# Rotary partners of the grouped tiles by transfers within SBUF in place of matmuls, two-part sums of squares, and a third buffer in the state-space stage

## The chip, the cores and the metric

The kernel runs on one core of one Trainium2 chip, in one launch. The metric is device time in microseconds, a median over runs; lower is better. The kernel before took 3017.12 us (median of three runs, 3015.85 to 3017.46). Engines are named as in the profile: PE does matmuls, PEld is its weight load, DVE is VectorE, ACT is ScalarE, POOL is GpSimd, and SP is SyncE, which here only issues transfers.

## What is computed

Two blocks stand one after the other on 512 tokens of width 1024. The first is a hybrid of dilated attention, pooling and a state-space scan, with a gated feed-forward part; the second is two layers of three parallel branches (differential attention, retention, grouped-query attention). All of it is fp32 data. Cut to what the change touches:

```python
# first block, state-space branch, per chunk of 128 tokens and per head
seg = a_cs[..., :, None] - a_cs[..., None, :]
Lmat = exp(where(causal, seg, -inf))

# second block, each of two layers
gq = axial_rope(rms_norm(gq, gqa_q_norm[l]))      # 8 heads of 64: 4 tiles of 128 rows
gk = axial_rope(rms_norm(gk, gqa_k_norm[l]))      # 2 heads of 64: 2 tiles (each head twice)
def apply_rope(x, cos, sin):                      # x1, x2: the halves of a group
    return concat([x1 * cos - x2 * sin, x2 * cos + x1 * sin])   # axial: halves of 16 in groups of 32
a = rms_norm(differential_attention(...), diff_subln[l], eps=1e-5)   # mean of squares over 128
r = head_group_norm(retention(...), ret_group_norm[l])               # variance over 128
```

## The kernel before

**Tiling.** Activations lie with features on the 128 partitions and the 512 tokens along the free dimension, so a tile is 128x512 fp32. A dense product with fp32 accuracy is made of three fp32r matmuls for each pair of 128-row blocks: both operands are split into a high part and the rest (uH, uL for activations, wH, wL for weights), and the products high x high, low x high and high x low are summed in PSUM. A weight tile of eight such blocks thus takes 24 matmuls. Weights come in chunks of up to 512 KB through four slots: SP loads a chunk into wR (`load`, which first waits in `ended` until the chunk four places earlier is used up), ACT rounds it to wH (`high`, three chunks ahead of the engine's place in its order), and DVE or POOL makes wL (`low`, `low_pool`).

**PSUM.** Of the eight banks, four are for the dense products and four for all else ("misc"). Both sets are given out in turn by an order that is written out ahead of time (`order_block1`, `order_layer`), and each user waits until the user four places earlier has released the bank.

**Order.** There is no scheduler. Each engine's instructions stand in the order in which the code issues them, and they meet at semaphores. Attention steps on PE are interleaved with eight dense matmuls at a time from a list of fill work (`fill`), and ACT and DVE follow the same marks.

**State-space stage (first block, 336 to 438 us).** For each of 16 groups of four heads DVE writes a 128x512 tile `ta` (`spread`) and POOL its low part `tl`; PE multiplies both with one triangular matrix (`seg`, L2073 and L2075), ACT takes the exponential into `dec`, DVE multiplies it with the chunk's scores (L2251), and PE uses the result (L2084) in `pair`. `ta` has two buffers, and `spread(n + 1)` stands ahead of group n's product on DVE.

**The grouped stage (each layer's start, "g"; 1144 to 1190 us in layer 0, 2080 to 2125 us in layer 1).** Six tiles are made one after the other (numbered 0 to 5 here in that order): the first four by two interleaved pairs of products, the last two by single ones; then comes the product of the grouped values, gv, in two half chunks, and then the grouped attention (`gqa_*`). For each tile ACT writes the scaled raw tile (`raw`, two buffers) and its squares (`sq`), and then counts up `raw_tile`. PE then sums the squares (L2796, `ss`) and makes the rotary partner (L2801, `rot`): a matmul with a signed permutation, both on full fp32 operands. DVE multiplies raw with the cosine (L2935), the partner with the sine (L2906), adds them (L2913), and multiplies with the root that ACT made of the sum (L2917), then counts up `rope_done`. Tile x + 2 may be written to `raw` when tile x has counted; the first attention scores wait for four tiles.

**The other rotary tiles.** The eight differential tiles ("d") and the eight retention tiles ("r") of a layer get their partners by transfers from `raw` to `partner` or `sg`, issued by SP in `swap_sp` right behind the load four chunks on: four of 8 partitions each for a "d" tile, two of 64 partitions for an "r" tile. All loads and swaps stand in one queue on SP.

**Means of squares.** Behind each of the four heads of the differential (`mean`, L3137) and retention (`var`, L3295) stages, ACT squares the head's output, and PE multiplies the squares with a matrix of ones, in full fp32.

## Time and profile before

| | |
|---|---|
| median of three runs | 3017.12 us |
| the profiled execution, its own time | 3017.55 us |
| its span in the trace | 3015.8 us |
| PE busy | 2946.7 us, 98% |
| weight loads busy | 2314.4 us, 77% |
| DVE busy | 1553.5 us, 52% |
| ACT busy | 1281.3 us, 42% |
| POOL busy | 452.7 us, 15% |
| mean granted PE clock | 0.996 of 2.4 GHz |

PE is busy throughout, and a matmul's bar in the trace overlaps its neighbours' bars, so what one costs is read from the distance between starts, not from its bar. In the lists, idle time before an instruction is followed by what ended it.

### The profile page before, as it was taken

What the parts mean: (1) busy time and instruction counts of PE and PEld (TensorE: products, weight loads), DVE (VectorE), ACT (ScalarE), POOL (GpSimd) and SP (SyncE); (2) the same over time, 40 slices, a digit from 0 to 9 for tenths busy, and PEclk for the clock granted to TensorE, in tenths of its full rate; (3) what the DMA queues carried; (4) which work ended last, traced back from release to release, by engine and by line L of the source; (5) the groups of instructions that cost most, each with busy time, mean ns of one, the idle gap of its engine ahead of it and who ended that gap; (6) DMA issues with size and microseconds to landing.
All of it is one profiled execution on the core that took longest, in us unless ns stands there. A gap on an engine that the chain in (4) does not pass through costs nothing. (4 is left out here: it accounts for less than half of the span.)

```text
span 3015.8 us, 36165 instructions
## 1 busy us (share of the span) xinstructions
PE 2946.7 (98%) x13328; PEld 2314.4 (77%) x13328; DVE 1553.5 (52%) x2058; ACT 1281.3 (42%) x1889; POOL 452.7 (15%) x264
## 2 busy tenths in 40 slices
PE   7999989999999999999999999999999999999999
PEld 6776778888778786677777888887667777888887
DVE  3427767445764666655634551435655743553241
ACT  3556325333542446655544432234655544332231
POOL 5000110000100002211112122121221111212121
PEclk9999999999999999999999999999999999999999
DMA  7322213333323332122322333333222322333332
GB/s 189 89 71 63 58 47 91 98 98 98 99 87 101 96 93 72 48 72 79 102 70 84 98 96 93 97 98 98 55 61 74 98 78 77 98 93 96 97 98 91
DMA packets 466355, 264.18 MB, mean 88 GB/s; under 512 B 21275, under 2 KB 455293, under 8 KB 466209
## 3 DMA queue, kind: packets, MB, share of 16 engines
q1 hardware_dynamic: 460256, 251.14, 28.9%
q0 software_dynamic: 5952, 11.13, 1.4%
q8 instruction: 87, 1.43, 0.2%
q14 instruction: 60, 0.48, 0.0%
HBM read 254.85 MB, written 5.64 MB: 86 GB/s over the span
## 5 line engine op out<-in xcount | busy, mean ns | idle before, releaser
L759 POOL TENSOR_TENSOR wL<-wR,wH 128x1024 fp32r<-128x1024 f32 (+1 forms) x159 | 386.7, 2433 | 2167.3 <-ACT wH L723 2167.3
L723 ACT ACTIVATE wH<-wR 128x1024 fp32r<-128x1024 f32 (+2 forms) x475 | 491.2, 1034 | 412.3 <-DMA wR<-in_w_mlp_out_dram 193.9
L728 DVE TENSOR_TENSOR wL<-wR,wH 128x1024 fp32r<-128x1024 f32 (+2 forms) x316 | 381.0, 1206 | 434.6 <-ACT wH L723 408.7
L790 PE MATMUL ps<-uH,wH 128*128 128x512 f32 x1200 | 486.5, 405 | 8.5 <-POOL wL L759 5.6
L790 PE MATMUL ps<-uL,wH 128*128 128x512 f32 x1200 | 483.5, 403 | 0.0
L790 PE MATMUL ps<-uH,wL 128*128 128x512 f32 x1200 | 479.9, 400 | 0.0
L778 PE MATMUL ps<-uH,wH 128*128 128x512 f32 x976 | 384.6, 394 | 7.3 <-DVE wL L728 5.7
L778 PE MATMUL ps<-uL,wH 128*128 128x512 f32 x976 | 379.9, 389 | 0.0
L778 PE MATMUL ps<-uH,wL 128*128 128x512 f32 x976 | 379.9, 389 | 0.0
L790 PEld LDWEIGHTS ps<-uH,wH 128*128 128x128 f32 x1200 | 227.3, 189 | 73.1 <-issue 16.8
L790 PEld LDWEIGHTS ps<-uL,wH 128*128 128x128 f32 x1200 | 227.7, 190 | 59.7 <-issue 15.4
L790 PEld LDWEIGHTS ps<-uH,wL 128*128 128x128 f32 x1200 | 227.4, 189 | 59.4 <-issue 13.8
L778 PE MATMUL ps<-mH,wH 128*128 128x512 f32 x688 | 268.1, 390 | 2.1 <-DVE wL L728 2.1
L778 PE MATMUL ps<-mH,wL 128*128 128x512 f32 x688 | 267.7, 389 | 0.0
L778 PE MATMUL ps<-mL,wH 128*128 128x512 f32 x688 | 267.7, 389 | 0.0
L778 PEld LDWEIGHTS ps<-uH,wH 128*128 128x128 f32 x976 | 183.2, 188 | 54.8 <-issue 10.4
L778 PEld LDWEIGHTS ps<-uL,wH 128*128 128x128 f32 x976 | 183.2, 188 | 38.7 <-issue 1.4
L778 PEld LDWEIGHTS ps<-uH,wL 128*128 128x128 f32 x976 | 183.2, 188 | 38.4
L778 PEld LDWEIGHTS ps<-mH,wH 128*128 128x128 f32 x688 | 129.1, 188 | 29.7 <-DVE wL L728 2.9
L778 PEld LDWEIGHTS ps<-mH,wL 128*128 128x128 f32 x688 | 129.1, 188 | 26.9
L778 PEld LDWEIGHTS ps<-mL,wH 128*128 128x128 f32 x688 | 129.1, 188 | 26.7
L3563 ACT ACTIVATE mH<-msc 128x512 f32 x64 | 40.5, 632 | 236.1 <-DVEq L3607 236.1
(476 smaller groups left out, 4173.4 us busy)
## 6 DMA issues: line engine op xcount, KB each, us to landing
wR<-in_w_in_dram SPq DMA_DIRECT2D x188, 512.0 KB, 3.7
wR<-in_w_mlp_in_dram SPq DMA_DIRECT2D x64, 512.0 KB, 4.0
wR<-in_w_mlp_out_dram SPq DMA_DIRECT2D x64, 512.0 KB, 3.6
wR<-in_ffn_w_up_dram SPq DMA_DIRECT2D x44, 512.0 KB, 3.8
wR<-in_w_branch_dram SPq DMA_DIRECT2D x24, 512.0 KB, 3.4
wR<-in_w_out_dram SPq DMA_DIRECT2D x16, 512.0 KB, 3.7
wR<-in_ffn_w_down_dram SPq DMA_DIRECT2D x16, 384.0 KB, 3.2
wR<-in_ffn_w_down_dram SPq DMA_DIRECT2D x16, 320.0 KB, 3.0
```

The costliest lines, as they stand in the source:

```text
L723: st.f(st.e.activation(wH[:, slot, 0:n], wR[:, slot, 0:n], ACT.Copy), hi_ready, c + 1)
L728: st.f(st.e.tensor_tensor(wL[:, slot, 0:n], wR[:, slot, 0:n], wH[:, slot, 0:n].bitcast(F32), ALU.subtract), lo_ready, c + 1 if done is Non ...
L759: e.tensor_tensor(wL[:, slot, 0:n], wR[:, slot, 0:n], wH[:, slot, 0:n].bitcast(F32), ALU.subtract).then_inc(sem("lo_pool"), 1)
L778: ins = pe.matmul(outp, w[:, k, c0:c0 + m], x[:, k0 + k, :], start=k0 == 0 and s == 0, stop=k0 + kt == kn and s == len(steps) - 1)
L790: ins = pe.matmul(o[:, :], w[:, k, :], x[:, k, :], start=s == 0, stop=s == 3 * KD - 1)
L3563: st.f(e.activation(mHf[:, ds((4 * i + j) * S, S)], msc[:, j % 2, :], ACT.Copy), sem("hidH_ready"), x + 1)
```

## The change

It has three parts. The first kernel of this call (the state-space stage belongs to it) gets a third `ta` buffer and one `spread` more ahead. In each layer of the second block the partners of the six grouped tiles are made by transfers that SP issues, eight of 16 partitions x 512 for a tile, into the buffer that the "d" tiles use later; the sine table's sign is moved into the table, the 12 `rot` matmuls and one memset per layer go, and ACT converts one weight chunk ahead of a root for the last two tiles. And the 16 sums of squares behind the heads are made of two fp32r matmuls each (high part and rest), for which ACT writes the square once more as fp32r and DVE subtracts; the order of ACT's copies is changed with it.

```diff
@@ -135,7 +135,7 @@
         for o, q in ((0, t // 64), (32, t % 64)):
             a = table(q, 32, 10000.0)
             out[2, b + o:b + o + 32, 0] = np.cos(np.concatenate([a, a]))
-            out[2, b + o:b + o + 32, 1] = np.sin(np.concatenate([a, a]))
+            out[2, b + o:b + o + 32, 1] = np.concatenate([-np.sin(a), np.sin(a)])
     return np.ascontiguousarray(out.reshape(3, P, 2 * S).astype(np.float32))
 
 
@@ -474,8 +474,6 @@
     def post(kind, t):
         if kind != "r":
             M.add("ss", kind, t)
-        if kind == "g":
-            M.add("rot", kind, t)
 
     def posts(kind):
 
@@ -1852,9 +1850,9 @@
     btok = kb("btok", [P, 4, 256], 58)
     dec = kb("dec", [P, 4, S], 70)
 
-    ta, tl = kb("ta", [P, 2, S], 78, F32R), kb("tl", [P, 2, S], 104, F32R)
-    gtR = kb("gtR", [P, P], 108, F32R)
-    avH, avL = kb("avH", [P, 4, 16], 108.5, F32R), kb("avL", [P, 4, 16], 108.75, F32R)
+    ta, tl = kb("ta", [P, 3, S], 99, F32R), kb("tl", [P, 2, S], 105, F32R)
+    gtR = kb("gtR", [P, P], 109, F32R)
+    avH, avL = kb("avH", [P, 4, 16], 109.5, F32R), kb("avL", [P, 4, 16], 109.75, F32R)
     xdd = kb("xdd", [P, S], 82)
     prev = kb("prev", [P, D], 88)
     ytok = kb("ytok", [P, D], 92)
@@ -2070,7 +2068,7 @@
             pe.wait_ge(sem("ta_ready"), n + 1)
             g = M("seg", n)
             o = g.open(pe)
-            pe.matmul(o[:, :], gtR[:, :], ta[:, n % 2, :], start=True, stop=False)
+            pe.matmul(o[:, :], gtR[:, :], ta[:, n % 3, :], start=True, stop=False)
             pe.wait_ge(sem("tl_ready"), n + 1)
             g.close(pe.matmul(o[:, :], gtR[:, :], tl[:, n % 2, :], start=False, stop=True))
 
@@ -2163,10 +2161,10 @@
 
         def spread(n):
             c, q = n // 4, n % 4
-            if n >= 2:
-                e.wait_ge(misc_ready, M("seg", n - 2).nth)
-            st.w()
-            st.s(e.tensor_tensor(ta[:, n % 2, :].rearrange("p (h t) -> p h t", h=4),
+            if n >= 3:
+                e.wait_ge(misc_ready, M("seg", n - 3).nth)
+            st.w()
+            st.s(e.tensor_tensor(ta[:, n % 3, :].rearrange("p (h t) -> p h t", h=4),
                                  C("le").unsqueeze(1).broadcast_to([P, 4, P]),
                                  avH[:, c, 4 * q:4 * q + 4].bitcast(F32).unsqueeze(2).broadcast_to([P, 4, P]), ALU.mult))
             st.w()
@@ -2219,6 +2217,7 @@
         follow("bt", 0)
         silu_dve(st, 11)
         spread(0)
+        spread(1)
         for c in range(4):
             follow("xt", c)
             for x in range(2):
@@ -2236,8 +2235,8 @@
                 st.w()
                 g.done(st, e.tensor_tensor(cbm[:, :, :], o[:, 0:256].rearrange("p (g t) -> p g t", g=2),
                                            C("le").unsqueeze(1).broadcast_to([P, 2, P]), ALU.mult))
-            if n + 1 < 16:
-                spread(n + 1)
+            if n + 2 < 16:
+                spread(n + 2)
             if n >= 2 and n % 2 == 0:
                 pair((n - 2) // 4, (n - 2) % 4 // 2)
             if n >= 5 and q == 1:
@@ -2672,7 +2671,7 @@
 
     XB = {"d": ("dq", "dk"), "r": ("rq", "rk"), "g": ("gq", "gk")}
 
-    HALVES = {"d": (8, (0, 64)), "r": (64, (0,))}
+    HALVES = {"g": (16, (0, 32, 64, 96)), "d": (8, (0, 64)), "r": (64, (0,))}
     ROPE = {"d": 0, "r": 1, "g": 2}
 
 
@@ -2681,6 +2680,7 @@
     sq = kb("sq", [P, 2, S], 4)
     rs = kb("rs", [P, 2, S], 8)
     partner = {"d": kb("partner", [P, 2, S], 12), "r": sg}
+    partner["g"] = partner["d"]
     qk = {"g": kb("qk_g", [P, 6, S], 92), "d": kb("qk_d", [P, 8, S], 64), "r": kb("qk_r", [P, 8, S], 16)}
     cs = {"g": kb("cs_g", [P, 2 * S], 106), "d": kb("cs_d", [P, 2 * S], 88), "r": kb("cs_r", [P, 2 * S], 60)}
     vv = {"gv": kb("vv_g", [P, NT, P], 104), "dv": kb("vv_d", [P, NT, S], 80), "rv": kb("vv_r", [P, NT, S], 100)}
@@ -2697,6 +2697,10 @@
     gst, ast = stt[:, 0], stt[:, 1]
     vsum = stt[:, 0, 0:2, :].rearrange("p a (t h) -> p (a t) h", h=4)
     rstd = nrmt
+
+    onesR = kb("onesR", [P, P], 112.5, F32R)
+    aoL, rqH = kb("aoL", [P, S], 110, F32R), kb("rqH", [P, S], 110, F32R)
+    rmH = rmL = at("rmH", [P, S], F32R, END - 8192 - 2048)
     hs = kb("hs", [P, S], 44)
     rg = kb("rg", [P, 4, S], 88)
     ro = kb("ro", [P, 2, S], 96)
@@ -2785,6 +2789,18 @@
                 e.sem_inc(sem("rv_ready"), 1)
             yield
 
+    def sums_of_parts_pe(pe, g, hi, lo):
+
+        o = g.open(pe)
+        pe.matmul(o[:, :], onesR[:, :], hi, start=True, stop=False)
+        g.close(pe.matmul(o[:, :], onesR[:, :], lo, start=False, stop=True))
+
+    def square_low(st, low, x, hi):
+
+        st.w()
+        st.s(st.e.tensor_tensor(low, x, hi.bitcast(F32), ALU.subtract))
+        st.w()
+
     def rope_post_pe(pe, kind, x, l):
 
         if kind == "r":
@@ -2794,15 +2810,10 @@
         g = M("ss", kind, t, l=l)
         o = g.open(pe)
         g.close(pe.matmul(o[:, :], C("blk64"), sq[:, x % 2, :], start=True, stop=True))
-        if kind != "g":
-            return
-        g = M("rot", kind, t, l=l)
-        o = g.open(pe)
-        g.close(pe.matmul(o[:, :], C("rot_g"), raw[kind][:, x % 2, :], start=True, stop=True))
-
     def partner_in(kind, x, l):
 
-        return 16 * (l * (4 * 4 + 4 * 2) + (4 * 4 if kind == "r" else 0) + (x // 2 + 1) * (4 if kind == "d" else 2))
+        return 16 * (l * (3 * 8 + 4 * 4 + 4 * 2) + {"g": 0, "d": 3 * 8, "r": 3 * 8 + 4 * 4}[kind] +
+                     (x // 2 + 1) * {"g": 8, "d": 4, "r": 2}[kind])
 
     def swap_sp(e, kind, x, l):
 
@@ -2819,10 +2830,13 @@
 
         o = orders(l)[0]
         x = o.names[name] - SLOTS
-        for kind in HALVES:
+        for kind in ("d", "r"):
             first = o.names[kind, TILES[kind][0]]
             if first <= x < first + KD:
                 swap_sp(e, kind, x - first, l)
+
+        for t in {3: (0, 1), 4: (2, 3), 5: (4,), 6: (5,)}.get(x - o.names["g", TILES["g"][0]], ()):
+            swap_sp(e, "g", t, l)
 
     def rope_pe(pe, kind, l):
 
@@ -2882,9 +2896,13 @@
                 g.done(st, e.activation(raw[kind][:, x % 2, :], o[:, :], ACT.Copy))
             st.w()
             e.sem_inc(sem("raw_tile"), 1)
+            late = kind == "g" and x > 3
+            if late:
+                high(st, (kind, t), l)
             if norm and x > 0:
                 root(x - 1)
-            high(st, (kind, t), l)
+            if not late:
+                high(st, (kind, t), l)
             yield
         if norm:
             root(len(order) - 1)
@@ -2898,17 +2916,10 @@
 
         def finish(x):
             y = qk[kind][:, order[x], :]
-            z = raw[kind][:, x % 2, :]
-            if kind == "g":
-                g = M("rot", kind, order[x], l=l)
-                o = g.take(e)
-                st.w()
-                g.done(st, e.tensor_tensor(z, o[:, :], table[:, S:2 * S], ALU.mult))
-            else:
-                z = partner[kind][:, x % 2, :]
-                e.wait_ge(sem(f"partner_in{x % 2}"), partner_in(kind, x, l))
-                st.w()
-                st.s(e.tensor_tensor(z, z, table[:, S:2 * S], ALU.mult))
+            z = partner[kind][:, x % 2, :]
+            e.wait_ge(sem(f"partner_in{x % 2}"), partner_in(kind, x, l))
+            st.w()
+            st.s(e.tensor_tensor(z, z, table[:, S:2 * S], ALU.mult))
             st.w()
             st.s(e.tensor_tensor(y, y, z, ALU.add))
             if norm:
@@ -2939,8 +2950,6 @@
                 finish(x - 1)
             if kind == "g" and x > 1:
                 low(st, (kind, t), l)
-            if kind == "g" and x == 3:
-                st.s(e.memset(partner["d"][:, :, :], 0.0))
             yield
         finish(len(order) - 1)
 
@@ -3131,10 +3140,8 @@
             g.close(ins)
 
         def mean(h):
-            pe.wait_ge(sem("aosq_ready"), 4 * l + h + 1)
-            g = M("on", h, l=l)
-            o = g.open(pe)
-            g.close(pe.matmul(o[:, :], C("ones"), ao[:, 1, :], start=True, stop=True))
+            pe.wait_ge(sem("aosq_low"), 4 * l + h + 1)
+            sums_of_parts_pe(pe, M("on", h, l=l), rmH[:, :], aoL[:, :])
         diff_steps(score, turned, value, mean, fill)
 
     def diff_act(st, l, follow):
@@ -3160,8 +3167,9 @@
                 if h:
                     e.wait_ge(sem("b_ready"), 27 + 20 * l + 4 + h)
                 st.w()
-                st.s(e.activation(ao[:, 0, :], o[:, :], ACT.Copy))
-                g.done(st, e.activation(ao[:, 1, :], o[:, :], ACT.Square))
+                st.s(e.activation(ao[:, 1, :], o[:, :], ACT.Square))
+                st.s(e.activation(rmH[:, :], o[:, :], ACT.Square))
+                g.done(st, e.activation(ao[:, 0, :], o[:, :], ACT.Copy))
                 st.w()
                 e.sem_inc(sem("aosq_ready"), 1)
             if 2 <= u < 18:
@@ -3219,6 +3227,11 @@
                     if u == 0:
                         e.wait_ge(sem("root_ready"), 3)
                     final_scale_dve(st, u)
+            if u >= 7 and u % 4 == 3 and u < 20:
+                h = u // 4 - 1
+                e.wait_ge(sem("aosq_ready"), 4 * l + h + 1)
+                square_low(st, aoL[:, :], ao[:, 1, :], rmH[:, :])
+                e.sem_inc(sem("aosq_low"), 1)
             if u >= 8 and u % 4 == 0:
                 h = u // 4 - 2
                 follow("on", h)
@@ -3289,10 +3302,8 @@
             g.close(ins)
 
         def var(h):
-            pe.wait_ge(sem("rsq_done"), 4 * l + h + 1)
-            g = M("rn", h, l=l)
-            o = g.open(pe)
-            g.close(pe.matmul(o[:, :], C("ones"), rsq[:, :], start=True, stop=True))
+            pe.wait_ge(sem("rsq_low"), 4 * l + h + 1)
+            sums_of_parts_pe(pe, M("rn", h, l=l), rqH[:, :], rmL[:, :])
         ret_steps(score, value, var, fill)
 
     def ret_act(st, l, follow):
@@ -3316,10 +3327,9 @@
             if h >= 2:
                 e.wait_ge(sem("b_ready"), 27 + 20 * l + 8 + h - 1)
             st.w()
-            st.s(e.activation(ro[:, h % 2, :], o[:, :], ACT.Copy))
-            g.done(st, e.activation(rsq[:, :], o[:, :], ACT.Square))
-            st.w()
-            e.sem_inc(sem("rsq_done"), 1)
+            st.s(e.activation(rsq[:, :], o[:, :], ACT.Square))
+            st.f(e.activation(rqH[:, :], o[:, :], ACT.Square), sem("rsq_done"), 4 * l + h + 1)
+            g.done(st, e.activation(ro[:, h % 2, :], o[:, :], ACT.Copy))
             follow("rn", h)
             g = M("rn", h, l=l)
             o = g.take(e)
@@ -3363,6 +3373,9 @@
                 st.w()
                 e.sem_inc(sem("rsc_ready"), 1)
             follow("ro", h)
+            e.wait_ge(sem("rsq_done"), 4 * l + h + 1)
+            square_low(st, rmL[:, :], rsq[:, :], rqH[:, :])
+            e.sem_inc(sem("rsq_low"), 1)
             follow("rn", h)
             x = ro[:, h % 2, :]
             e.wait_ge(sem("rrt_ready"), 4 * l + h + 1)
@@ -3449,6 +3462,8 @@
         rest(fill.parts)
 
     def layer_dve(st, l):
+        if l == 0:
+            st.s(st.e.tensor_copy(onesR[:, :], C("ones")))
         normed_u_dve(st, u_base("normed", l), 1 + l, lambda k: lp[:, k:k + 1], 2 + 3 * l,
                      lambda: low(st, ("g", TILES["g"][0]), l))
         low(st, ("g", TILES["g"][1]), l)
```

SP, at the start of the grouped stage of layer 0, kernel before: `wR` is the weight buffer, the 128x4x128 loads are the two half chunks of gv, and the 128x8x128 ones belong to the "d" tiles.

```order
L716 DMA wR<-in_w_in_dram 128x4x128 x2
L716 DMA wR<-in_w_in_dram 128x8x128 x5
L2816 DMA partner<-raw 8x512 x4
L716 DMA wR<-in_w_in_dram 128x8x128
L2816 DMA partner<-raw 8x512 x4
```

The same place in the changed kernel:

```order
L714 DMA wR<-in_w_in_dram 128x4x128 x2
L2827 DMA partner<-raw 16x512 x16
L714 DMA wR<-in_w_in_dram 128x8x128
L2827 DMA partner<-raw 16x512 x16
L714 DMA wR<-in_w_in_dram 128x8x128
L2827 DMA partner<-raw 16x512 x8
L714 DMA wR<-in_w_in_dram 128x8x128
L2827 DMA partner<-raw 16x512 x8
L714 DMA wR<-in_w_in_dram 128x8x128 x2
L2827 DMA partner<-raw 8x512 x4
```

Forty-eight transfers have moved in between the loads of the second gv half and of the third "d" chunk, each row of them behind a wait for its tiles.

DVE, at the start of the state-space stage, before (`ta` is `spread`, `xdt` and `cbm` are the products with which a chunk begins):

```order
L1991 SCALAR_TENSOR_TENSOR xc_105<-xc_105,cvt 128x512
L2169 TENSOR_TENSOR ta<-cn,avH 128x512
L728 TENSOR_TENSOR wL<-wR,wH 128x1024
L2228 TENSOR_TENSOR xdt<-ps,dts 128x512 x2
L728 TENSOR_TENSOR wL<-wR,wH 128x1024
L2228 TENSOR_TENSOR xdt<-ps,dts 128x512 x6
L2237 TENSOR_TENSOR cbm<-ps,cn 128x256
L2169 TENSOR_TENSOR ta<-cn,avH 128x512
```

and in the changed kernel:

```order
L1989 SCALAR_TENSOR_TENSOR xc_105<-xc_105,cvt 128x512
L2167 TENSOR_TENSOR ta<-cn,avH 128x512 x2
L726 TENSOR_TENSOR wL<-wR,wH 128x1024
L2227 TENSOR_TENSOR xdt<-ps,dts 128x512 x2
L726 TENSOR_TENSOR wL<-wR,wH 128x1024
L2227 TENSOR_TENSOR xdt<-ps,dts 128x512 x6
L2236 TENSOR_TENSOR cbm<-ps,cn 128x256
L2167 TENSOR_TENSOR ta<-cn,avH 128x512
```

The second `ta` stands at the start, and each later one is one group further on than it was, at the same places.

DVE, between the scores of a differential step and the mean of the second head of layer 0, in the changed kernel (L3222 reduces the scores, `qk_r` and `sg` belong to a retention tile):

```order
L3222 TENSOR_REDUCE stt<-ps 128x1 x2
L2946 TENSOR_TENSOR qk_r<-raw_r,cs_r 128x512
L2922 TENSOR_TENSOR sg<-sg,cs_r 128x512
L2924 TENSOR_TENSOR qk_r<-qk_r,sg 128x512
L2801 TENSOR_TENSOR aoL<-ao,rmH 128x512
L2946 TENSOR_TENSOR qk_r<-raw_r,cs_r 128x512
```

L2801 is new; the rows around it stood in this order before.

## Rows read from the trace of the kernel before

**Rows 1.** The page: busy time of each engine, share of the span, instructions.

```profile
PE 2946.7 (98%) x13328; PEld 2314.4 (77%) x13328; DVE 1553.5 (52%) x2058; ACT 1281.3 (42%) x1889; POOL 452.7 (15%) x264
```

**Rows 2.** Groups by line: names, shapes, count | busy us, mean ns | idle before.

```profile
L2801 PE MATMUL ps<-raw,cn 128*128 128x512 f32 x24 | 12.2, 592 | 0.0
...
L3295 PE MATMUL ps<-nrmt,cn 128*128 128x512 f32 x16 | 8.2, 590 | 0.0
L3137 PE MATMUL ps<-ao,cn 128*128 128x512 f32 x16 | 8.2, 590 | 0.0
```

**Rows 3.** PE's waits, whole span: total us, times, longest us.

```profile
PE ps L2073 <- DVEq L2173: 5.7, 3, 2.9
PE ps L790 <- POOL wL L759: 5.6, 2, 2.8
...
PE ps L2084 <- DVEq L2253: 2.6, 2, 1.9
```

**Rows 4.** Timeline of PE, grouped stage, layer 0: start us, us, operation.

```profile
1155.79 1.02 PE L2801 MATMUL ps<-raw,cn 128*128 128x512 f32 x2
1156.65 1.02 PE L2796 MATMUL ps<-sq,cn 128*128 128x512 f32 x2
...
1157.96 0.79 PE L790 MATMUL ps<-uH,wH 128*128 128x512 f32 x1
```

**Rows 5.** Timeline of PE around the mean of a differential head.

```profile
1389.33 0.39 PE L790 MATMUL ps<-uH,wH 128*128 128x512 f32 x1
1389.55 1.02 PE L3137 MATMUL ps<-ao,cn 128*128 128x512 f32 x2
1390.50 1.13 PE L3007 MATMUL ps<-qk_d 64*128 64x256 f32 x8
```

**Rows 6.** Timeline of DVE between scores and mean, second head.

```profile
1423.52 0.69 DVE L2913 TENSOR_TENSOR qk_r<-qk_r,sg 128x512 f32<-128x512 f32 x1
```

**Rows 7.** Timeline of PE, state-space stage: two waits for `ta`.

```profile
408.14 0.50 PE L2073 MATMUL ps<-ta,gtR 128*128 128x512 f32 x1 [1.59 <-DVEq L2173]
...
421.88 0.50 PE L2073 MATMUL ps<-ta,gtR 128*128 128x512 f32 x1 [2.89 <-DVEq L2173]
```

**Rows 8.** Windows: stretch, us, busy by engine (instructions), granted clock, DMA share, GB/s.

```profile
405.00:415.00 10.00, 8.41 (x41) 6.84 (x41) 5.61 (x8) 2.55 (x4) 1.04 (x1) 0.83 0.18 53
420.00:430.00 10.00, 8.12 (x35) 6.55 (x36) 5.32 (x9) 3.03 (x5) 0.00 (x0) 0.83 0.19 52
...
2120.00:2130.00 10.00, 8.79 (x36) 6.28 (x36) 5.71 (x7) 4.09 (x9) 6.71 (x3) 0.83 0.00 0
```

**Rows 9.** By tile, SP's issues: count: least, median, longest ns.

```profile
L2816 SPq DMA_DIRECT2D partner<-raw x64: 624/625/1059, 1193.7 to 2215.8; - x64
...
L2816 SPq DMA_DIRECT2D sg<-raw_r x32: 461/564/2072, 1407.6 to 2403.0; - x32
```

**Rows 10.** Timeline of SP: first loads of the stage; swaps of a "d" tile.

```profile
1154.45 1.05 SPq L716 DMA_DIRECT2D wR<-in_w_in_dram  x2
...
1204.11 2.64 SPq L2816 DMA_DIRECT2D partner<-raw  x4
```

**Rows 11.** DMA issues: count, KB each, median us to landing.

```profile
cn<-table_consts_dram SPq DMA_DIRECT2D x1, 64.0 KB, 1.9
```

**Rows 12.** Timeline, grouped stage, layer 0: DVE and ACT.

```profile
1156.92 0.69 DVE L2906 TENSOR_TENSOR raw<-ps,cs_g 128x512 f32<-128x512 f32 x1
...
1159.22 0.69 ACT L2879 ACTIVATE raw<-ps,lp 128x512 f32<-128x512 f32 x1 [1.71 <-DVEq L2919]
...
1163.63 1.23 DVE L728 TENSOR_TENSOR wL<-wR,wH 128x1024 fp32r<-128x1024 f32 x1
```

**Rows 13.** Timeline, start of grouped attention, layer 0: DVE, then ACT, then PE.

```profile
1188.75 1.49 DVE L3105 TENSOR_REDUCE stt<-ps 128x1 f32<-128x512 f32 x2
...
1190.33 0.69 ACT L3071 ACTIVATE gpr<-ps,stt 128x512 f32<-128x512 f32 x1 [3.44 <-DVEq L3107]
...
1192.71 0.49 PE L3007 MATMUL ps<-qk_g 64*128 64x256 f32 x2
```

## The prediction

> **What bounds the kernel now.** I read the busy table first: PE is busy 98% of the span, DVE and ACT half of it [rows 1]. So PE's own order is the path nearly everywhere, a matmul taken out of it is worth its full place, and an edit on another engine counts only where PE comes to wait for it. Then the list of PE's waits: small ones, and three of them lie in stages that the change touches, 5.7 us at L2073 for `ta`, 2.6 us at L2084 for DVE's product with `dec`, and 5.6 us (twice 2.8) where the first fill matmul of a layer's grouped attention waits for POOL's low part of a weight chunk [rows 3]. Then the timelines of those places, for what is late next. The sum is made against the profiled execution (3017.55 us, 1.75 us over its span); it stands 0.4 us over the median 3017.12, so I add the differences to the median.
>
> **What a matmul costs.** In the timeline an fp32 product of 128x512 appears as two records, and the next product starts 0.86 us after it (1155.79 to 1156.65) [rows 4]. A dense fp32r matmul starts 0.22 us ahead of its successor (1389.33 to 1389.55), and the mean behind a head holds PE for 0.95 us until the next product (1389.55 to 1390.50), of which some 0.09 us is that product's own start [rows 5].
>
> **Part 1, the sums of squares.** L3137 and L3295 have 16 records each, so 16 products in all [rows 2]. Each goes from 0.86 us to two fp32r matmuls, 0.45 us: 0.41 us less, and 16 x 0.41 = 6.5 us. It needs an extra ACT pass (0.6 us) and a DVE subtraction (0.69 us, as DVE's L2913 [rows 6]) ahead of PE's product. For the second head of layer 0 the subtraction stands behind the L2913 that ends at 1424.2 [rows 6]; it would be ready near 1425.0, and PE's product comes two matmul groups later, at 1428.1. I went through all eight places of layer 0 in the same way; the tightest is the last differential head, about 1 us ahead of PE. So no wait takes the place of the gain, and I take -6.5 us, with 0 as the bound if DVE is late everywhere. Queued behind DVE's new waits are weight conversions; only the one behind the last differential head moves by much (some 8 us), and its chunk is two chunks from use.
>
> **Part 2, the first kernel.** PE waits for `ta` three times. With a third buffer and the same places on DVE, `ta` is there one group early and all three waits go. What is late next differs. At the first (the remaining 1.2 us, near 395 us) DVE works without a gap and PE waits 1.9 us for its product with `dec` a few microseconds on, the longest of the L2084 waits [rows 3]: the wait moves there, gain 0. At the second (1.6 us, 408.14) the next product has its operand, so 1.6 us is gained [rows 7]; the granted clock was 0.83 over 405 to 415 us, thus 10 x 0.17 = 1.7 us of full-speed work lost, and with PE fed it should stay up [rows 8]. I count 1.6 + 1.5 = 3.1 us. At the third (2.9 us, 421.88) [rows 7] the next half pair needs DVE's product, which comes behind one `ta` and two additions of some 0.7 us each, and holds PE again: of 2.9 us plus the 1.7 us of clock in 420 to 430 us [rows 8] I count 2.1 us. Sum -5.2 us; bounds 0 (DVE holds PE at all three) and -9 us (all waits 5.7 and both clock losses 3.4).
>
> **Part 3, the grouped partners.** Off PE go 12 products (24 records [rows 2]) of 0.86 us, 10.3 us, 5.2 us in each layer. In their place SP issues eight transfers for a tile, one after the other. The trace of before has no transfer of 16 partitions; the nearest are those of 8 partitions, median 625 ns, and of 64, median 564 ns [rows 9]. Four of the first take 2.64 us, 0.66 us apart [rows 10]. I take 0.66, as 16 is nearer to 8 than to 64; the bounds are 0.46, the shortest within SBUF, and 0.8, since single ones took 1.06 and 2.07 us [rows 9]. From issue to landing 64 KB take 1.9 us [rows 11]; for the last of a tile I take 2.1. So a tile's partner lands 7 x 0.66 + 2.1 = 6.7 us after its first issue.
>
> Now the walk through layer 0. The load ahead of the swaps is issued near 1155.1 [rows 10], so tile 0's transfers run from 1155.8 and land at 1162.5, tile 1's from 1161.1, landing at 1167.8. Before, DVE had tile 0's partner at 1156.92, and ACT wrote raw tile 2 at 1159.22 [rows 12]: 2.3 us of DVE lie between. Now raw tile 2 is written at 1164.8 to 1166.1. PE's first dense matmul started at 1157.96 behind both partners [rows 4]; now it starts 0.86 us earlier (not 1.7, as tile 1's squares are not ready sooner), and 24 matmuls, 5.8 us with the slower first, bring it to 1162.9. It needs tile 2's squares: **a new wait of 3.3 us**. Tile 5's product needs the low part of its weight chunk, which DVE makes (L728) only behind the finish of tile 1: before at 1163.63 [rows 12], now from 1170.1 to 1171.4. PE, free at 1167.2, waits until 1171.6, **another 4.4 us**. After such gaps I expect a lower clock: in layer 1 it was 0.83 over 2120 to 2130 us behind a 2.8 us wait [rows 8]; I add 1.2 us. SP goes on behind: tiles 2 and 3 land at 1173.8 and 1179.1, tile 4 at 1185.9, tile 5 at 1191.9. Those do not hold the next products for more than 0.6 us, since ACT now converts one chunk ahead of the root; and the 2.8 us wait for POOL [rows 3] goes, because PE comes late for it anyway. The first scores start at 1188.9. But DVE has tile 5 to finish ahead of the first maximum: 1191.9 + 2.2 = 1194.1, where it was 1188.75, and ACT's exponentials, which free the PSUM bank that the second scores need, end at 1196.5 instead of 1191.0 [rows 13]. PE starts those scores at 1196.7, against 1192.71 [rows 13]: **layer 0 is 4.0 us slower**, and the 5.2 us of removed products are used up. In layer 1 the same walk gives 0.5 us less, and the clock loss of before (10 x 0.17 us in 2120 to 2130 [rows 8]) mostly has its place in the new waits: +2.4 us. Together +6.4 us; at 0.46 us an issue the same walk gives about -1 us a layer, at 0.8 us some 6 us a layer more.
>
> One page of the Trainium skill speaks against this part: DMA: Bandwidth & Descriptors, section Rules for kernel authors, says to coalesce small transfers and that under 64 KB one mostly pays overhead; these are 32 KB. The same page, section Anatomy of one DMA, puts the sequencer's share at about 50 ns (for the GpSimd path): by that, an estimate, a tile's eight issues would be 0.4 us, both waits would nearly vanish, and part 3 would be worth most of its 10.3 us. The 0.66 us between starts [rows 10] is against the small share.
>
> **Sum.** -6.5 - 5.2 + 6.4 = -5.3 us, 3011.8. Waits of 2 to 4 us follow each other in the grouped stage, and a second low-clock stretch there is about as likely as not in one layer (1.7 us at the most); I round up to **3012.0 us**.
>
> **Rivals.** *(a) The transfers hide.* If SP issues them at 0.46 us, part 3 gives -2 us: 3017.1 - 6.5 - 5.2 - 2 = 3003.4 us; if an issue costs next to nothing, part 3 gives some -9 us, 2996.4 us. Range 2996 to 3006. For it: some issues within SBUF took 0.46 us; against it: the medians of 0.56 and 0.63 us [rows 9]. 0.12, of which 0.03 for the lower value. That lower value is what the page named above would give. *(b) The swap queue holds PE longer, and the kernel is slower than before.* Place: SP's queue, 48 transfers a layer. From 0.66 to 0.8 us an issue each tile comes 1.1 us later, the six in series 6 us a layer, +12: 3024 us. The point where the gain of the other parts is used up is about 0.72 us an issue (5.3 us of the 12 us that 0.14 us cost). For it: single issues of up to 1.06 and 2.07 us [rows 9]; against it the medians. The same sign comes about if two clock losses fall in each layer. 0.18, range 3017 to 3030. *(c) The first kernel gives nothing*, since DVE, not `ta`, holds PE at all three places; the L2084 wait [rows 3] shows that it does at one: 3017 us, range 3014 to 3018. 0.15. The forecast itself, 0.55, with a range of 3005 to 3017.
>
> **Range and chances.** 3003.5 to 3020.5 us leaves out most of (a) and the upper half of (b), together under 0.2. A measurement of this kernel can tell about 0.2% (6 us) from no change. Faster by more than that (under 3011.1): (a), and somewhat over half of the forecast's case, 0.41. Slower by more (over 3023.1): half of (b), 0.09. Within: 0.50.
>
> **What would show it.** In the profile of the changed kernel: L2801 and L3137/L3295 gone from PE, 32 fp32r matmuls in their place, 0.22 us apart and with no wait ahead of them (part 1). No PE wait at `seg`; a longer one at the `dec` products near 400 and 424 us, and a granted clock near 1 from 405 to 430 us (part 2). SP's 48 swaps per layer some 0.66 us apart; PE waits of 3 us ahead of the sum of squares of the third tile and of 4 us ahead of tile 5's product, released by ACT and by DVE's wL; a clock dip right there; and DVE's first maximum some 5 us later (part 3). What would make me wrong: an issue spacing under 0.5 or over 0.75 us, or low-clock stretches that come or go elsewhere.

## The result and the profile after

| | before | changed |
|---|---|---|
| median, 13 runs each | 3017.11 us (3013.93 to 3020.54) | 3022.47 us (3018.28 to 3026.57) |
| ratio, 95% interval | | 1.0018 (1.0009 to 1.0026) |
| span of the profiled execution | 3015.8 us | 3016.5 us |

The change makes the kernel 5.4 us slower, where I had forecast 5 us faster; the time is 2 us above the top of my range. The trace needs care: the profiled execution of the changed kernel took 3018.28 us, the least of its 13 runs, with a mean granted clock of 0.993; the median of the runs' clocks is 0.990. Among the 13, 0.001 of clock goes with 1.5 us. So the trace shows where the time goes, but less of it than the usual run has.

From the page of the changed kernel, the busy times (PE's is 12 us less than in [rows 1]), and then lines of the list of PE's waits (us in total, times, longest):

```profile
PE 2934.4 (97%) x13304; PEld 2311.1 (77%) x13304; DVE 1567.6 (52%) x2073; ACT 1288.7 (43%) x1905; POOL 453.1 (15%) x264
```

```profile
PE ps L788 <- DVE wL L726: 11.5, 5, 4.2
PE ps L3016 <- ACT gpr L3080: 8.2, 4, 3.8
...
PE ps L2812 <- ACTq L2898: 6.3, 2, 3.2
PE ps L2082 <- DVEq L2252: 5.8, 3, 3.2
```

Against [rows 3], the waits for `ta` and for POOL are gone. One group is new, the wait for the squares of a tile (L2898), and three have grown: for the low part of weights (L726 is DVE's `low`; 2.9 us before), for the exponentials of the first scores (L3080; 0.7 us before), and for DVE's product with `dec` (L2252; 2.6 us before). The timeline of PE in layer 0's grouped stage shows the first three of them in order (L2812 is the sum of squares, L788 dense, L3016 scores):

```profile
1149.72 1.02 PE L2812 MATMUL ps<-sq,cn 128*128 128x512 f32 x2
...
1160.64 1.23 PE L2812 MATMUL ps<-sq,cn 128*128 128x512 f32 x2 [3.15 <-ACTq L2898]
1166.12 0.79 PE L788 MATMUL ps<-uH,wH 128*128 128x512 f32 x1 [4.24 <-DVE wL L726]
1166.71 0.63 PE L788 MATMUL ps<-uL,wH 128*128 128x512 f32 x1
1167.13 0.63 PE L788 MATMUL ps<-uH,wL 128*128 128x512 f32 x1
...
1194.12 1.13 PE L3016 MATMUL ps<-qk_g 64*128 64x256 f32 x8 [3.73 <-ACT gpr L3080]
...
1201.53 1.13 PE L3016 MATMUL ps<-qk_g 64*128 64x256 f32 x8
```

```profile
1154.93 1.02 PE L2796 MATMUL ps<-sq,cn 128*128 128x512 f32 x2
...
1198.51 1.13 PE L3007 MATMUL ps<-qk_g 64*128 64x256 f32 x8
```

The second fence is the kernel before, with the same first and last event (the first sum of squares and the third scores): 43.6 us lie between them there, 51.8 in the changed kernel, so layer 0's stage costs 8.2 us more. Layer 1 costs 5.5 more (from 2090.23 to 2140.87 us, before 2090.83 to 2135.99). What releases PE is on SP and DVE (L2827 is the swap, L2922 to L2928 the finish of a tile, L3114 the maximum of the scores), with POOL's low parts (L757) below:

```profile
1150.32 10.39 SPq L2827 DMA_DIRECT2D partner<-raw  x16
...
1161.38 11.30 SPq L2827 DMA_DIRECT2D partner<-raw  x16
```

```profile
1157.08 0.69 DVE L2922 TENSOR_TENSOR partner<-partner,cs_g 128x512 f32<-128x512 f32 x1 [5.51 <-DMA partner<-raw]
...
1164.84 1.22 DVE L726 TENSOR_TENSOR wL<-wR,wH 128x1024 fp32r<-128x1024 f32 x1 [0.50 <-DVE qk_g L2928]
...
1187.06 0.81 DVE L2922 TENSOR_TENSOR partner<-partner,cs_g 128x512 f32<-128x512 f32 x1 [2.59 <-DMA partner<-raw]
1187.90 2.78 DVE L2924 TENSOR_TENSOR qk_g<-qk_g,partner 128x512 f32<-128x512 f32 x1
1190.79 0.69 DVE L2928 TENSOR_TENSOR qk_g<-qk_g,rs 128x512 f32<-128x512 f32 x1
1191.62 1.48 DVE L3114 TENSOR_REDUCE stt<-ps 128x1 f32<-128x512 f32 x2
```

```profile
1184.94 5.19 POOL L757 TENSOR_TENSOR wL<-wR,wH 128x1024 fp32r<-128x1024 f32 x2 [2.54 <-ACT wH L721]
```

Tile 0's partner is used 6.8 us after the first issue, and 16 issues take 10.39 us, 0.65 us each. The granted clock (the third column from the end), in windows of the changed kernel:

```profile
1165.00:1171.00 6.00, 4.88 (x12) 3.82 (x13) 4.69 (x5) 2.55 (x5) 1.71 (x1) 0.50 0.26 57
1190.00:1200.00 10.00, 6.28 (x30) 4.87 (x29) 7.54 (x10) 6.20 (x13) 2.51 (x2) 0.83 0.22 60
```

Behind the waits of 3.15 and 4.24 us PE has 0.50, the 1.2 GHz level, and its matmuls start 0.42 us apart (1166.71 to 1167.13) in place of 0.23.

The means are as intended, two fp32r matmuls 0.23 us apart, without a wait:

```profile
1392.58 0.39 PE L2795 MATMUL ps<-rmH,onesR 128*128 128x512 f32 x1
1392.81 0.39 PE L2796 MATMUL ps<-aoL,onesR 128*128 128x512 f32 x1
```

### The profile page after: what moved, and what is told of

It is laid out like the page before. It is cut to its first block and busy times, and to the rows that moved or that the text cites. A ratio compares the mean times of both kernels' runs of the same rounds, so it can differ in the third digit from the quotient of the medians.

```text
span 3016.5 us, 36263 instructions
## 1 busy us (share of the span) xinstructions
PE 2934.4 (97%) x13304; PEld 2311.1 (77%) x13304; DVE 1567.6 (52%) x2073; ACT 1288.7 (43%) x1905; POOL 453.1 (15%) x264
## 5 line engine op out<-in xcount | busy, mean ns | idle before, releaser
L757 POOL TENSOR_TENSOR wL<-wR,wH 128x1024 fp32r<-128x1024 f32 (+1 forms) x159 | 386.9, 2434 | 2170.8 <-ACT wH L721 2170.7
L726 DVE TENSOR_TENSOR wL<-wR,wH 128x1024 fp32r<-128x1024 f32 (+2 forms) x316 | 380.5, 1204 | 419.4 <-ACT wH L721 392.2
L788 PE MATMUL ps<-uH,wH 128*128 128x512 f32 x1200 | 486.1, 405 | 12.1 <-DVE wL L726 11.5
L788 PE MATMUL ps<-uL,wH 128*128 128x512 f32 x1200 | 481.8, 402 | 0.0
L788 PE MATMUL ps<-uH,wL 128*128 128x512 f32 x1200 | 479.6, 400 | 0.0
L776 PE MATMUL ps<-uH,wH 128*128 128x512 f32 x976 | 384.7, 394 | 7.1 <-DVE wL L726 5.6
L776 PE MATMUL ps<-uH,wL 128*128 128x512 f32 x976 | 380.0, 389 | 0.0
L776 PE MATMUL ps<-uL,wH 128*128 128x512 f32 x976 | 380.0, 389 | 0.0
L788 PEld LDWEIGHTS ps<-uH,wH 128*128 128x128 f32 x1200 | 227.8, 190 | 78.6 <-issue 16.7
L788 PEld LDWEIGHTS ps<-uL,wH 128*128 128x128 f32 x1200 | 228.0, 190 | 58.4 <-issue 13.9
L788 PEld LDWEIGHTS ps<-uH,wL 128*128 128x128 f32 x1200 | 227.3, 189 | 58.1 <-issue 12.5
L776 PE MATMUL ps<-mH,wH 128*128 128x512 f32 x688 | 268.1, 390 | 2.1 <-DVE wL L726 2.1
L776 PE MATMUL ps<-mH,wL 128*128 128x512 f32 x688 | 267.7, 389 | 0.0
L776 PE MATMUL ps<-mL,wH 128*128 128x512 f32 x688 | 267.6, 389 | 0.0
L776 PEld LDWEIGHTS ps<-uH,wH 128*128 128x128 f32 x976 | 183.2, 188 | 54.6 <-issue 10.4
L776 PEld LDWEIGHTS ps<-uL,wH 128*128 128x128 f32 x976 | 183.2, 188 | 38.7 <-issue 1.4
L776 PEld LDWEIGHTS ps<-uH,wL 128*128 128x128 f32 x976 | 183.2, 188 | 38.4
L776 PEld LDWEIGHTS ps<-mH,wH 128*128 128x128 f32 x688 | 129.1, 188 | 29.7 <-DVE wL L726 2.9
L776 PEld LDWEIGHTS ps<-mL,wH 128*128 128x128 f32 x688 | 129.1, 188 | 26.8
L776 PEld LDWEIGHTS ps<-mH,wL 128*128 128x128 f32 x688 | 129.1, 188 | 26.7
```

The source lines that it names most:

```text
L726: st.f(st.e.tensor_tensor(wL[:, slot, 0:n], wR[:, slot, 0:n], wH[:, slot, 0:n].bitcast(F32), ALU.subtract), lo_ready, c + 1 if done is Non ...
L757: e.tensor_tensor(wL[:, slot, 0:n], wR[:, slot, 0:n], wH[:, slot, 0:n].bitcast(F32), ALU.subtract).then_inc(sem("lo_pool"), 1)
L776: ins = pe.matmul(outp, w[:, k, c0:c0 + m], x[:, k0 + k, :], start=k0 == 0 and s == 0, stop=k0 + kt == kn and s == len(steps) - 1)
L788: ins = pe.matmul(o[:, :], w[:, k, :], x[:, k, :], start=s == 0, stop=s == 3 * KD - 1)
```

## Experiments

All ratios are against the kernel before, run beside them; n is the number of runs. An interval is mostly 3 us to each side, so two kernels whose medians differ by 2 us are not told apart by the times alone; there I say what the trace shows. In the expectations, the theory and its rival are named with a time each; the text behind a time says which of them it fits.

### Each part alone

**Without the transfers**, parts 1 and 2. All of part 3 is undone; its core:

```diff
+        g = M("rot", kind, t, l=l)
+        o = g.open(pe)
+        g.close(pe.matmul(o[:, :], C("rot_g"), raw[kind][:, x % 2, :], start=True, stop=True))
...
-        for t in {3: (0, 1), 4: (2, 3), 5: (4,), 6: (5,)}.get(x - o.names["g", TILES["g"][0]], ()):
-            swap_sp(e, "g", t, l)
```

> The changed kernel with the grouped partners back on PE: parts 1 and 2 of the change, nothing of part 3. Theory A (the transfers cost what the trace after shows, 8.2 us in the first layer and 5.2 in the second, most of it waits of PE followed by a stretch at the lower clock): the means give their 7.0 and the state-space part some 3.5, so 3017.1 - 10.5 = 3006.6 us, ratio 0.9965. Rival B (part 3 costs 6.4 us as predicted, and what is missing was lost in parts 1 or 2): 3022.5 - 6.4 = 3016 us. No half-clock stretch in the grouped stage under A.

Measured: 3010.39 us, 0.9980 (0.9971 to 0.9989), n 11. Part 3 thus costs 12.1 us within the change by the medians (11.6 by the ratios). That is nearer to theory A's 13.4 than to rival B's 6.4. The time itself lies 3.8 us above theory A's 3006.6, since A counted 3.5 us for part 2, which gives nothing (below).

**Part 3 alone**: of the diff of the change, the hunks on `rot`, `HALVES`, `partner_in`, `swaps_sp`, `late` and `finish`.

> The kernel before with part 3 alone, the partners of the grouped tiles by transfers. Theory A: 3017.1 + 13.4 = 3030.5 us, ratio 1.0044, with waits near 3.2, 4.2 and 3.7 us at the same three places of each layer and 10 us at half clock behind the first two. Rival B: 3017.1 + 6.4 = 3023.5 us.

Measured: 3027.27 us, 1.0041 (1.0028 to 1.0055), n 5: 8 to 17 us slower than the kernel before. This fits theory A, and rival B (my +6.4) falls. The waits in layer 0 are 3.09, 3.76 and 3.73 us.

**Part 2 alone**: the hunks on `ta`, `seg` and `spread`.

> The kernel before with part 2 alone, the third buffer of the state-space segments and its first kernel. By the trace after it gives 3.5 us: 3013.6 us. By the prediction 5.2: 3011.9 us. The rival, that it gives nothing since another wait of the same length takes the place: 3017 us. The trace is to show whether the half-clock stretch at 397 to 404 us comes with this part alone.

Measured: 3018.61 us, 1.0008 (0.9999 to 1.0017), n 11. Part 2 gives nothing that can be measured, as its rival had it. PE and DVE of this kernel, then the same places before:

```profile
399.80 1.10 PE L2084 MATMUL ps<-xdt,dec 128*128 128x64 f32 x8 [3.16 <-DVEq L2254]
```

```profile
398.99 0.69 DVE L2252 TENSOR_TENSOR dec<-dec,cbm 128x512 f32<-128x512 f32 x1
```

```profile
394.92 0.50 PE L2073 MATMUL ps<-ta,gtR 128*128 128x512 f32 x1 [1.26 <-DVEq L2173]
...
400.27 1.10 PE L2084 MATMUL ps<-xdt,dec 128*128 128x64 f32 x8 [1.95 <-DVEq L2253]
```

```profile
399.46 0.69 DVE L2251 TENSOR_TENSOR dec<-dec,cbm 128x512 f32<-128x512 f32 x1
```

DVE makes its product for `dec` at 398.99 us in place of 399.46, since it works with gaps of 0.24 us at the most from 390 us on, whatever PE does. PE's two waits, 1.26 and 1.95 us, have become one of 3.16. In all, PE waits 3.2 us less over the stage (8.6 to 5.4), but the clock falls. The first two windows are this kernel's, the third is the kernel before:

```profile
395.00:405.00 10.00, 6.84 (x28) 4.49 (x27) 7.69 (x12) 0.15 (x1) 0.64 (x2) 0.83 0.00 0
420.00:430.00 10.00, 8.08 (x24) 6.13 (x25) 5.39 (x8) 2.69 (x3) 0.00 (x0) 0.66 0.19 52
```

```profile
395.00:405.00 10.00, 8.05 (x39) 6.20 (x40) 8.34 (x11) 1.20 (x2) 2.08 (x2) 1.00 0.01 2
```

Before, it was 1.00 in 395 to 405 us, and 0.83 both in 405 to 415 and in 420 to 430 [rows 8]. This one trace does not account for the whole loss: from the first L1021 product behind the last L2052 to the stage's last product (L2106) it takes 101.3 us, the kernel before 103.7, and the kernel with part 1 alone, whose stage is the same as before, 102.0. What takes these 2.3 us away in the usual run is told by the runs' clock, whose median is 0.992 where the kernel before had 0.996 beside it, and by the filled kernel below.

**Part 1 alone**: the hunks on `sums_of_parts_pe` and `square_low`.

> The kernel before with part 1 alone, the means as two single-pass products of a high and a low part. By the prediction and by the trace after: 3017.1 - 6.5 to 7.0 = 3010.1 to 3010.6 us, ratio 0.9978, and no wait of PE for aosq_low or rsq_low. The rival, that the extra ACT and DVE steps cost PE elsewhere: above 3013 us.

Measured: 3010.26 us, 0.9981 (0.9972 to 0.9990), n 11: as forecast, and no wait of PE for the new steps is in its list. The three parts alone, by their medians, give -6.4 + 2.0 + 10.7 = +6.3 us, near the +5.4 of all together.

### Is it the clock?

**Filled waits in the state-space part.** In `pair` (dummy results land in the next group's bank, which its own product then overwrites):

```diff
+            if c > 0:
+                o2 = M("yo", c, x).open(pe)
             for r in range(2):
+                if r == 1:
+                    for _ in range({(2, 0): 14, (3, 0): 8}.get((c, x), 0)):
+                        pe.matmul(o2[:, :], gtR[:, :], uH[:, 0, :], start=True, stop=True)
                 pe.wait_ge(sem("m_ready"), n + r + 1)
```

> Part 2 alone (3018.6 us), with 14 and 8 such matmuls ahead of the two products of the state-space part at which PE waited 3.16 us (at 399.8 us) and 1.93 us (at 421.9). Clock theory: the half-clock stretches of 3.4 us at 401 and 6.8 us at 422 go, which cost some 1.7 + 3.4 us, so 3013.5 us, which is what the waits alone had promised. Rival (part 2 loses what it gives for another reason): 3018.6 us.

Measured: 3014.95 us, 0.9994 (0.9985 to 1.0003), n 11; median clock 0.996 again.

```profile
395.00:405.00 10.00, 10.00 (x49) 7.58 (x48) 8.18 (x12) 0.63 (x2) 2.02 (x2) 1.00 0.01 2
```

This is 3.7 us less than part 2 alone, by work that computes nothing: the clock theory, at three quarters of the expected size. Even so, part 2 then gives only about 2 us, which its interval (4.5 us faster to 0.9 slower) does not tell from nothing.

**Filled waits in the grouped stage.** 32 such matmuls ahead of tile 2's sum of squares, 16 between the opening of the two banks of the second scores.

```diff
+        if kind == "g" and x == 2:
+            spend(pe, o, 32)
         pe.wait_ge(sem("raw_tile"), rope_base(kind, l)[0] + x + 1)
...
+        outs = [groups[0].open(pe)]
+        spend(pe, outs[0], 16 if u == 1 else 0)
+        outs.append(groups[1].open(pe))
```

> The changed kernel with matmuls that compute nothing wanted put into the two stretches in which PE only waits in the grouped stage of each layer: 32 ahead of the squares of tile 2 (3.15 + 4.24 us of waits) and 16 ahead of the second scores (3.73 us). Their results are overwritten by the product that follows. All that PE waits for is unchanged. Clock theory (a wait costs its length once more in part, since the granted clock falls to half behind it and the products there take 0.43 us in place of 0.23): the stretches at half clock behind 1161 and 1195 us go, 2.6 + 1.5 us per layer, so 3022.5 - 8.2 = 3014.3 us. Rival (the fall of the clock is an accident of its own and costs nothing here): 3022.5 us or a little above.

Measured: 3018.09 us, 1.0002 (0.9993 to 1.0011), n 11, 4.4 us less than the changed kernel; median clock 0.995 in place of 0.990.

```profile
1157.00:1175.00 18.00, 10.61 (x32) 7.27 (x30) 11.30 (x15) 8.48 (x13) 1.71 (x1) 0.72 0.29 74
```

```profile
1157.00:1175.00 18.00, 16.43 (x71) 12.92 (x70) 9.72 (x12) 7.24 (x11) 1.71 (x1) 1.00 0.31 77
```

The clock theory again, at half size (4.4 of 8.2 us). The first fence is the changed kernel. With the clock full throughout, the stage takes 49.5 us to the third scores, 2.3 less than 51.8. Of the 2.6 us that 13 products at the front had lost (0.43 us apart in place of 0.23), 1.2 come back at the second scores (43.2 us after the first squares in place of 44.4), since DVE and the transfers set those; 1.1 come back behind them. The 1.2 us pass through SP's queue: in the changed kernel the load ahead of tile 4's transfers waits for its slot from 1172.7 to 1174.5 us, with the waits filled only 0.5 us.

**Parts 1 and 2, filled, and then one wait more.** The first has the 14 and 8 matmuls; the second also 12 behind the last grouped tile, where PE waits 2.8 us for POOL as it did before the change [rows 3].

> Parts 1 and 2 (3010.4 us), with the 14 and 8 idle-time matmuls of the run before in the state-space part. If the fall of the clock behind the two waits there is what cancels part 2, it gives 3.7 us here too: 3006.7 us. Rival, that parts 1 and 2 together lose it elsewhere: 3010.4 us.

> As the kernel with parts 1 and 2 and the filled state-space waits (3007.6 us), and 12 more matmuls in the 2.80 us in which PE waits for POOL's low part behind the last grouped tile, in each layer. If the clock falls because of that wait, the half-clock stretches of 3.4 us at 1181 and 2116 us go, 1.7 us each: 3004.2 us. Rival: 3007.6 us.

Measured: 3007.63 us, 0.9967 (0.9956 to 0.9978), n 7, and 3005.26 us, 0.9959 (0.9945 to 0.9972), n 5. Windows of the first, then of the second:

```profile
1176.00:1190.00 14.00, 11.20 (x43) 7.46 (x43) 8.70 (x11) 7.86 (x13) 8.25 (x3) 0.88 0.12 34
```

```profile
1176.00:1190.00 14.00, 13.88 (x58) 9.38 (x57) 8.36 (x11) 7.87 (x13) 8.36 (x3) 1.00 0.15 43
```

The clock is 1.00 in place of 0.88. The times, -2.8 and -2.4 us, lie on the side of the theory, each by itself within the intervals; together, against parts 1 and 2 unfilled, they are 5.1 us.

### What holds the grouped stage?

**Weights ahead.** The high part of the sixth tile's weights goes ahead of ACT's wait for `rope_done`, its low part ahead of DVE's `finish(0)`.

```diff
+            if kind == "g" and x == 2:
+                high(st, (kind, t), l)
             if x >= 2:
                 e.wait_ge(sem("rope_done"), b + x - 1)
...
+            if kind == "g" and x == 1:
+                low(st, (kind, order[2]), l)
             if x > 0:
                 finish(x - 1)
```

> The changed kernel with the high and low part of the weights of the sixth grouped tile made before PE and DVE wait for the partners (ACT's step ahead of its wait for the first finished tile, DVE's ahead of that tile). The wait of 4.24 us for that low part goes. Theory that the chain of transfers, ACT and DVE is what bounds the stage: PE meets it a few steps later, at the weights of the values' second half, whose low part stands behind the fourth partner, and only 2.1 us per layer come back, 3018.3 us. Rival, that the wait was the weights' alone: 4.24 + 2.6 us of clock per layer come back, 3008.9 us.

Measured: 3025.28 us, 1.0025 (1.0014 to 1.0035), n 8.

```profile
1182.80 0.53 PE L776 MATMUL ps<-uH,wH 128*128 128x512 f32 x1 [2.84 <-DVE wL L726]
```

The wait of 4.24 us is gone, and PE waits 2.84 us at the values' second half (L776), as the chain theory had it, with the clock down behind it. Almost nothing comes back: PE's waits in the stage are 1.7 us shorter in sum, the stage takes 51.5 us in place of 51.8, and the clock takes the rest (0.83 over 1180 to 1190 us). So the 2.1 us that I expected did not come, and the rival is out. That the kernel is 2.8 us slower than the changed one is hardly clear of the spread of the runs, and I did not settle it.

**Half of the issues to ACT.** The weights ahead, and in `rope_act`, with `swap_sp` left the first two of the four groups of partitions:

```diff
             e.sem_inc(sem("raw_tile"), 1)
+            if kind == "g":
+                swap_part(e, "g", x, (64, 96))
```

> As the kernel with the weights ahead, and half of each grouped tile's transfers issued by ACT in place of SP, so that a partner takes 4 issues in a row in place of 8 (SP's took 0.65 us each). Theory that the issues bound the stage: the first partner lands 2.6 us sooner, the second 5.2; the waits of 3.15 and 3.73 us fall to under 1.5 us each, and the kernel comes near what the products of PE taken away promise: 3022.5 less 13.4 (the loss of part 3 in the trace after) less up to 10.3 gives a floor of 2998.8; I expect 3004 to 3010 us. Rival (ACT's own issues hold up its steps of the stage as long as SP's did): 3016 us or above. ACT's price for an issue is unknown here.

Measured: 3036.04 us, 1.0064 (1.0050 to 1.0078), n 5, as the rival had it. ACT's own timeline (ACTq is its queue):

```profile
1168.76 2.67 ACTq L2833 DMA_DIRECT2D partner<-raw  x4
1171.48 0.69 ACT L880 ACTIVATE rs<-ps,cn 128x512 f32<-128x512 f32 x1 [2.81 <-issue]
```

Four issues hold ACT for 2.67 us, 0.67 each, the same as on SP, and the root behind them, on which DVE's finish hangs, comes as much later. This chain is longer than the one it was to shorten.

**Two and four transfers a tile in place of eight.** The diff is that of two; four are (32, (0, 64)). The bytes are the same, but these kernels leave out the rotary order of the rows: whole halves or quarters change places, so they do not compute the model, and only their time is read.

```diff
-    HALVES = {"g": (16, (0, 32, 64, 96)), "d": (8, (0, 64)), "r": (64, (0,))}
+    HALVES = {"g": (64, (0,)), "d": (8, (0, 64)), "r": (64, (0,))}
```

> The changed kernel with each grouped tile's rows sent by 2 transfers of 64 partitions in place of 8 of 16: the same bytes and waits, a quarter of the issues. The rows that arrive are not the rotary partners, so the computation is changed and only its time is read. Theory that SP's issues bound the stage (0.65 us each, so 5.2 us per tile and 31 of the 37 us from the first issue to the last partner): the first partner lands 3.6 us sooner, the waits of 3.15, 4.24 and 3.73 us fall below 1 us each, and so does the clock's loss behind them: near 3010.4 (parts 1 and 2 alone) less the 10.3 of the products, 3000 to 3003 us. Rival, that the landing of a transfer and the round ACT, SP, DVE, ACT for each pair of tiles bound it whatever the number of issues: 3015 us or above.

> The changed kernel with 4 transfers of 32 partitions per tile in place of 8 of 16 (again rows that are not the partners, so its time alone is read). With 8 issues it takes 3022.5 us, with 2 it took 3015.0. If the time of the issues is what is lost, the 4 lie between: by a straight line, 3022.5 - 4 x 1.25 = 3017.5 us. Rival, a threshold (once the first partner lands before PE needs it, fewer issues bring nothing): 3015 us.

Measured: 3014.97 us, 0.9995 (0.9986 to 1.0004), n 11, and 3015.14 us, 0.9991 (0.9982 to 1.0000), n 11. So the issues cost 7.4 us of part 3's 12. The times alone do not tell a straight line (3017.5 for four) from a threshold (3015), but the traces do: with four and with two a tile PE's waits in layer 0 are the same, 0.61, 3.64 and 3.14 us, and the stage takes 46.8 and 46.7 us. Both kernels come out at their rivals' 3015 us, though the number of issues did matter. Two long waits are left with two transfers a tile; its PE:

```profile
1164.76 0.80 PE L788 MATMUL ps<-uH,wH 128*128 128x512 f32 x1 [3.64 <-DVE wL L726]
...
1192.01 1.14 PE L3016 MATMUL ps<-qk_g 64*128 64x256 f32 x8 [3.14 <-ACT gpr L3080]
```

3.64 us for the weights of the sixth tile, which stand behind tile 0 and 1 on ACT and DVE, and 3.14 us at the second scores. With 12 products fewer on PE and partners that are early, this is still 4.6 us slower than parts 1 and 2 without transfers.

**Two transfers, weights ahead.** Both edits together, with the same rows left out.

> As the kernel with two transfers of 64 partitions per tile (3015.0 us; not the rotary partners' rows, so its time alone is read), and the sixth tile's weights made ahead of the waits for the partners. The wait of 3.64 us for that low part goes. Theory that with few issues the chain follows PE: the 3.6 us and the 2.6 us at half clock behind them come back in each layer, 3015.0 - 12 = 3003 us, with 3 us of waiting left at the second scores. Rival, that PE meets another wait further on, as it did with all transfers: 3012 us or above.

Measured: 3014.64 us, 0.9990 (0.9981 to 0.9999), n 11, as the rival had it. The 3.64 us are gone, and PE waits 2.64 us at the values' second half (1177.66 us) and 3.17 at the second scores.

**The first two tiles' partners on PE, the other four by transfers** (on part 1 alone). In the first kernel the transfers of the third tile stand in SP's queue behind the load they stood behind in the change; in the second they are ahead of it:

```diff
-        for t in {4: (2, 3), 5: (4,), 6: (5,)}.get(...):
+        for t in {3: (2,), 4: (3,), 5: (4,), 6: (5,)}.get(...):
```

> Part 1 (3010.3 us) with the transfers for the last four grouped tiles of each layer only; the first two have their partners from a product on PE, as before. No part 2. Theory that it is the 16 issues in a row at the stage's start that hold up the chain, and that 32 issues in a layer are hidden: four products of 0.86 us per layer go and no wait comes, 3010.3 - 6.9 = 3003.4 us. Rival, that the later tiles' transfers hold PE as well (the second scores wait for the last partner): 3010 us or above.

> As the kernel with the first two tiles' partners on PE (3018.6 us), with the transfers of the third tile issued ahead of the weight load behind which SP's queue held them, and the fourth's ahead of the next load. In the trace of that kernel the third tile's rows were there at 1159.4 us and SP issued them from 1163.65 on. Theory, queue and end of the stage: the third and fourth partners land 4 to 5 us sooner, the wait of 5.70 us for the weights' low part falls to some 1.4 us, the wait of 3.16 us for the second scores stays, since DVE and ACT set that; 6 to 7 us come back in the first layer and 4 to 5 in the second, so 3007 to 3012 us, no better than part 1 alone (3010.3). Rival, that the queue was all that stood against hidden transfers: 3003.4 us.

Measured: 3018.61 us, 1.0004 (0.9995 to 1.0013), n 11, and 3009.96 us, 0.9978 (0.9968 to 0.9988), n 9. The first fits its rival, the second its theory (3007 to 3012). SP of the first shows why:

```profile
1153.37 9.94 SPq L716 DMA_DIRECT2D wR<-in_w_in_dram  x3
1163.65 11.10 SPq L2833 DMA_DIRECT2D partner<-raw  x16
```

The third tile's rows are ready at 1159.4 us, but the load ahead of them waits until 1163.3 for its slot. Moving the issue ahead of it gives 8.7 us: its place in SP's queue was worth about as much as the number of issues (7.4), within the intervals. The second kernel is only level with part 1 alone (3010.26 us), although eight products, by my price 6.9 us, are off PE. PE of the second kernel, then its DVE and POOL at the end of the stage (here L2934 to L2940 are the finish):

```profile
1176.94 0.67 PE L778 MATMUL ps<-uH,wH 128*128 128x512 f32 x1 [2.15 <-DVE wL L728]
1194.23 2.08 PE L3028 MATMUL ps<-qk_g 64*128 64x256 f32 x8 [3.74 <-ACT gpr L3092]
```

```profile
1185.23 2.74 DVE L2934 TENSOR_TENSOR partner<-partner,cs_g 128x512 f32<-128x512 f32 x1 [0.67 <-DMA partner<-raw]
1188.01 2.78 DVE L2936 TENSOR_TENSOR qk_g<-qk_g,partner 128x512 f32<-128x512 f32 x1
...
1191.73 1.49 DVE L3126 TENSOR_REDUCE stt<-ps 128x1 f32<-128x512 f32 x2
```

```profile
1185.04 5.20 POOL L759 TENSOR_TENSOR wL<-wR,wH 128x1024 fp32r<-128x1024 f32 x2 [4.12 <-ACT wH L723]
```

The wait at the second scores is left, 3.74 us, and its cause is seen: while POOL makes two low parts, DVE's steps of 0.69 us take 2.74 and 2.78 us. In the kernel before, POOL worked at the same place:

```profile
1182.57 8.29 POOL L759 TENSOR_TENSOR wL<-wR,wH 128x1024 fp32r<-128x1024 f32 x3 [14.23 <-ACT wH L723]
```

```profile
1183.19 0.69 DVE L2906 TENSOR_TENSOR raw<-ps,cs_g 128x512 f32<-128x512 f32 x1
1183.91 1.89 DVE L2913 TENSOR_TENSOR qk_g<-qk_g,raw 128x512 f32<-128x512 f32 x1
```

There the partner's product with the sine (L2906) reads PSUM and takes 0.69 us; the slow steps have both inputs in SBUF (L2913, 1.89 us). With the transfer, the partner lies in SBUF, and that step can be held up too. The Trainium skill, SBUF — State Buffer, section SBUF: two separate sides, states the rule: DVE, with both inputs in SBUF, and a GpSimd instruction that reads SBUF share a pair of ports, and the later one is blocked for the whole of the other. The trace agrees: 2.74 us against 0.69 for this step, and in the changed kernel the step of 2.78 us, begun at 1187.90, ends 0.55 us behind POOL's second low part (1190.13).

**The two low parts by DVE.** e16 on the kernel above, e17 with part 2 and its filled waits as well, e18 on the changed kernel.

```diff
+KEPT = {_o[0].names["d", _t] for _o in ORDERS[1:] for _t in TILES["d"][1:3]}
 def by_pool(x):
-    return x in BESIDE or x >= FIRST and x % 2 == 1
+    return x not in KEPT and (x in BESIDE or x >= FIRST and x % 2 == 1)
...
+        rest(g)
         low(st, ("gv", 1), l)
-        rest(g)
```

> As the kernel with part 1 and the transfers of four tiles, issued early (3010.0 us), with two of POOL's low parts of the weights in each layer (those of the second and third differential tile) made by DVE, the second of them behind the last grouped tile. Collision theory: DVE's steps beside them fall from 2.7 to 0.69 us, the two low parts cost DVE 1.23 us each, the maximum of the first scores starts 2.5 us sooner, and the wait of 3.74 us for the second scores falls to 1.2 us with 1.7 us of clock behind it: 3010.0 - 8 = 3002 us. Rival, that DVE's own extra work takes the place of the collision: 3010 us.

> The kernel before this one with part 2 and its filled waits as well. What that gave without transfers was 3010.4 - 3007.6 = 2.8 us, or some 2.7 us against part 1 alone: 2999 us by the collision theory, 3007 us by its rival. Without transfers the best kernel so far takes 3005.3 us.

> The changed kernel with the same two low parts by DVE and nothing else. The waits of 3.15 and 4.24 us at the front of the stage stay, since the transfers set them. Collision theory: the last tile's three steps end 2.4 us sooner, and the wait of 3.73 us for the second scores is shorter by as much, with up to 1.7 us of clock behind it: 3022.5 - 5 to 8 = 3014 to 3018 us. Rival: 3022.5 us.

Measured: e16 3007.72 us, 0.9966 (0.9952 to 0.9979), n 5; e17 3003.32 us, 0.9955 (0.9942 to 0.9969), n 5; e18 3020.63 us, 1.0012 (1.0003 to 1.0021), n 11. DVE of e16, then its PE:

```profile
1187.27 0.69 DVE L2939 TENSOR_TENSOR qk_g<-qk_g,partner 128x512 f32<-128x512 f32 x1
...
1189.43 1.23 DVE L731 TENSOR_TENSOR wL<-wR,wH 128x1024 fp32r<-128x1024 f32 x1
1190.76 1.49 DVE L3129 TENSOR_REDUCE stt<-ps 128x1 f32<-128x512 f32 x2
```

```profile
1193.26 1.13 PE L3031 MATMUL ps<-qk_g 64*128 64x256 f32 x8 [2.58 <-ACT gpr L3095]
```

Without POOL beside it DVE is back at 0.69 us, which shows the collision. But DVE's own low part of 1.23 us stands ahead of the maximum, and the wait falls only from 3.74 to 2.58 us. The times, -2.2 us for e16 and -1.8 for e18 against the kernels that they were made from, are a third or less of what I expected and within the intervals: e16 and e18 came out nearer to their rivals (DVE's extra work takes the collision's place), e17 half-way between. So the collision is shown in the steps, and what it costs the kernel is not shown by a time. Layer 0's stage takes 46.5 us in the kernel above, 44.3 in e16, and 43.6 before the change, with all partners on PE. e17 is the fastest kernel of the study, 13.6 us (9 to 18) under the kernel before; e14, without transfers, has 12.4 (8 to 17), so that transfers beat the products is not shown.

## Why the prediction was wrong

**Part 1** was right: -6.5 forecast, -5.7 us (-8.4 to -3.0) measured alone; no wait came.

**Part 2** failed at the clock's recovery, the 1.5 in "I count 1.6 + 1.5 = 3.1 us" and what of it stands in the 2.1 us of the third wait. -5.2 was forecast; alone, +2.4 us (-0.3 to +5.1) came, and beside part 1, +0.1 (3010.39 against 3010.26). The waits themselves went nearly as I had counted them: in the trace of part 2 alone the 1.6 us at the second place are gone, of the 2.9 at the third 1.9 are left, and 0.6 behind it are gone, 3.2 us in all. The clock went the other way. That the first wait would move to DVE's product I had seen, and I booked it at 0; but there two short waits became one of 3.16 us, the clock fell behind it, where it had been 1.00, and it fell to 0.66 in 420 to 430 us. Filling the waits gave back 3.7 us. "A granted clock near 1 from 405 to 430 us" held in the changed kernel's trace, which has 0.66 in 395 to 405 us instead, and not in that of the part alone; a sum must not rest on one execution's clock.

**Part 3**, +6.4 forecast, +12.1 us measured within the change. The steps of its front came as forecast: 0.65 us an issue (0.66), 6.8 us to the first partner (6.7), waits of 3.15 and 4.24 us (3.3 and 4.4), POOL's wait gone. What failed is the end of the walk, "1191.9 + 2.2 = 1194.1", and the clock behind it. In the trace of layer 0 these terms close the sum:

- The second scores. I had them 1196.7 - 1154.9 = 41.8 us after the first squares; they came at 1194.12 - 1149.72 = 44.4, so 2.6 us later. 2.1 of it is one DVE step of 2.78 us in place of 0.69 beside POOL; I had priced DVE's finish at its undisturbed 2.2 us, although POOL's work there was in the trace.
- The clock behind the second scores: 1.6 us, which I had only as a chance. With the 4.0 us of the forecast, 4.0 + 2.6 + 1.6 = 8.2 us.
- Layer 1: +2.4 forecast, +5.5 in the trace, for the same reasons.

That is 13.7 us of loss in the trace for 6.4. The clock at the front I set at 1.2 us; the matmuls there lost 2.6, of which 1.2 reach the second scores (the filled kernel), since those wait for DVE.

Taken one after the other, by medians, part 1 gives -6.9 us, part 2 on top of it +0.1, and part 3 on top of both +12.1, together the +5.4 of the change. The forecasts were -6.5, -5.2 and +6.4.

**Many small transfers.** The eight issues a tile cost 7.4 us against two or four. The advice of the Trainium skill that I had weighed (DMA: Bandwidth & Descriptors, section Rules for kernel authors), to coalesce small transfers, was right in direction. The 50 ns for the sequencer, which section Anatomy of one DMA gives for the GpSimd path, do not describe an issue here, at 0.65 us on SP.

**Rivals.** (a) fell: the issues take 0.65 us. (b) had the right sign, and by luck its range: its mechanism, slower issues, did not occur. Its remark that two clock losses in each layer give the same sign has both stretches of the trace on its side, but not DVE's slower step, 2.1 us a layer. (c) was right on part 2's time, but not on its reason: DVE held PE at two of the three places, and the second wait did go. I gave it 0.15 as if the other parts would hold: part 2's +2 with part 3's forecast would give 3019, inside the range. The range missed since the failures of parts 2 and 3 add up, and I had treated them as alternatives.

**Open.** The time of the weights-ahead kernel; how much of part 3's 12 us the clock takes in a usual run (the filled kernel gives back 4.4); what the collision of DVE and POOL costs the kernel; and whether an earlier place for DVE's low part would make the transfers pay. No run here shows it.

## What to carry to other kernels

A product taken off a busy engine is worth its time only up to the next thing that engine waits for. Read what is late next at the end of the stage, not only where the edit is: here the second scores left 1.5 us of room (in the changed kernel PE starts them 0.9 us after ACT's first exponential, 1193.20 to 1194.12 us; before, that exponential started at 1190.33 and PE only at 1192.71 [rows 13], so 1.5 us were left), and 5.2 us of products a layer were taken away.

Waits merge. Two waits of 1 to 2 us that become one of 3 us can cost what their removal promised, since the granted clock falls behind the long one; matmuls that compute nothing, put into such waits, gave back 3.7 and 4.4 us in two kernels, and 5.1 in two steps in a third. The median granted clock of the runs belongs beside every time.

An operand moved from PSUM to SBUF changes what DVE collides with, and a transfer is as late as the load that it stands behind.

## What the runs showed of the hardware

- An issue of a transfer within SBUF, back to back, takes 0.65 us on SP and 0.67 on ACT, and on ACT it holds the activations behind it (2.81 us of idle for four).
- A transfer of 16, 32 or 64 partitions makes no difference to the time of its issue that I could find: in layer 0's grouped stage the median is 589 ns for the 48 issues of 16 partitions (523 to 1822), 590 for the 24 of 32 (507 to 628), and 592 for the 12 of 64 (461 to 799).
- DVE's fp32 step of 0.69 us takes up to 2.8 us beside a POOL instruction of 2.4 to 2.9 us when both of its inputs are in SBUF, and ends some 0.5 us behind it; the same step with an input from PSUM, and the reduction from PSUM, do not slow down (0.69 us, and 1.49 us for two).
- With the same instructions the mean granted clock varies from run to run, and the time with it: 0.993 to 0.989 and 3018.3 to 3026.6 us for the changed kernel.
- The granted clock fell to 0.50, the 1.2 GHz level, behind waits of 3.15 and 4.24 us in an otherwise busy stretch, and stayed at 1.00 there when the waits were filled.
